# Recurrence gates as products of 64 rows in both halves of the rows, and the heads' sums of squares by high and low part

## The reference

```python
xb = uc.reshape(B, T, 16, 64)                      # 16 blocks of 64 channels
r_gate = sigmoid(einsum('btnc,ncd->btnd', xb, w_r) + b_r)
i_gate = sigmoid(einsum('btnc,ncd->btnd', xb, w_i) + b_i)
log_a = -8.0 * r_gate * softplus(-lru_lambda); a = exp(log_a)
u = sqrt(-expm1(2 * log_a)) * (i_gate * uc)        # then h_t = a_t h_{t-1} + u_t
...
o = attention(q1, q2, k1, k2, v)                   # 8 heads of 128 values
o = o * rsqrt(mean(o * o, axis=-1) + EPS) * g_sub  # per head: the sum of squares
```

## Time and profile before

| | us |
|---|---|
| median of 3 runs | 1968.31 |
| lowest and highest run | 1966.69, 1970.43 |
| the profiled execution | 1966.05 |
| its span from first to last instruction | 1963.2 |
| mean granted TensorE clock in it | 0.996 of full speed |
| PE busy | 1920.9 (98%) |
| DVE busy | 1277.0 (65%) |
| ACT busy | 1061.2 (54%) |
| POOL busy | 191.1 (10%) |

### The profile page before, as it was taken

How to read it: one execution, slowest core, us unless ns; L and a number is a source line. 1 busy time by engine, 2 the same in 40 slices (tenths; PEclk the granted TensorE clock), 3 DMA queues, 4 the chain that set the end, 5 groups by cost and what they waited for, 6 DMA issues and landing times.

```text
span 1963.2 us, 37319 instructions
## 1 busy us (share of the span) xinstructions
PE 1920.9 (98%) x15214; PEld 1880.6 (96%) x15214; DVE 1277.0 (65%) x2334; ACT 1061.2 (54%) x1715; POOL 191.1 (10%) x242
## 2 busy tenths in 40 slices
PE   7999999999999999999999999999999999999997
PEld 7999999999998999999989999999999999999997
DVE  6667676765437766666667676767644388666666
ACT  6466666665236644444565757575732475444445
POOL 4312121100110000000041212120001000000000
PEclk9999999999999999999999999999999999999998
DMA  5323232222332332333313232322232323332221
GB/s 140 105 66 108 71 96 71 85 76 75 93 101 65 99 95 87 86 97 96 98 55 101 66 105 70 103 81 75 76 86 86 97 71 92 92 112 88 87 90 65
DMA packets 275709, 172.32 MB, mean 88 GB/s; under 512 B 7592, under 2 KB 271104, under 8 KB 275552
## 3 DMA queue, kind: packets, MB, share of 16 engines
q1 hardware_dynamic: 268000, 155.47, 27.0%
q0 software_dynamic: 7520, 14.59, 2.4%
q10 hardware_dynamic: 32, 0.04, 0.0%
HBM read 158.86 MB, written 11.21 MB: 87 GB/s over the span
## 4 chain that ended last, share of the span: by engine, by line
PE 87%; ACT 6%; DVE 4%; issue 2%; DMA 0%; SPq 0%; ACTq 0%; DVEq 0%
PE PJ L778 37%; PE PJ L1054 19%; PE PX L1115 13%; PE PJ L960 5%; PE PJ L790 3%; PE PX L989 2%; PE PX L1007 1%; PE PX L902 1%; PE PX L1027 1%; ACT w_hi L1286 1%; PE PX L790 1%; DVE T L1951 1%; PE PX L892 1%; DVE Y L1873 1%; DVE X L1876 1%
## 5 line engine op out<-in xcount | busy, mean ns | idle before, releaser
L1841 DVE TENSOR_TENSOR w_lo<-w_raw,w_hi 128x1024 fp32r<-128x1024 f32 x236 | 299.1, 1269 | 187.7 <-ACT w_hi L1286 186.6
L1286 ACT ACTIVATE w_hi<-w_raw 128x1024 fp32r<-128x1024 f32 x236 | 247.4, 1052 | 204.4 <-DMA w_raw<-in_w_down 120.3
L778 PE MATMUL PJ<-h_hi,w_hi 128*128 128x272 f32 x1536 | 328.4, 295 | 2.6 <-DVE T L1951 1.9
L778 PE MATMUL PJ<-h_hi,w_lo 128*128 128x272 f32 x1536 | 316.6, 288 | 0.0
L778 PE MATMUL PJ<-h_lo,w_hi 128*128 128x272 f32 x1536 | 315.9, 287 | 0.0
L778 PEld LDWEIGHTS PJ<-h_hi,w_hi 128*128 128x128 f32 x1536 | 239.5, 189 | 10.8 <-issue 8.8
L778 PEld LDWEIGHTS PJ<-h_lo,w_hi 128*128 128x128 f32 x1536 | 240.4, 188 | 0.0
L778 PEld LDWEIGHTS PJ<-h_hi,w_lo 128*128 128x128 f32 x1536 | 240.0, 189 | 0.0
L1054 PE MATMUL PJ<-u_hi,w_hi 128*128 128x272 f32 (+2 forms) x1016 | 215.8, 288 | 0.0
L1054 PE MATMUL PJ<-u_hi,w_lo 128*128 128x272 f32 (+2 forms) x1016 | 214.3, 288 | 0.0
L1054 PE MATMUL PJ<-u_lo,w_hi 128*128 128x272 f32 (+2 forms) x1016 | 213.9, 287 | 0.0
(11 more groups left out here) (409 smaller groups left out, 4760.9 us busy)
## 6 DMA issues: line engine op xcount, KB each, us to landing
w_raw<-in_w_in SPq DMA_DIRECT2D x110, 512.0 KB, 3.7
w_raw<-in_w_down SPq DMA_DIRECT2D x64, 512.0 KB, 3.6
w_raw<-in_w_up SPq DMA_DIRECT2D x62, 512.0 KB, 5.2
w_raw<-in_w_branch_attn SPq DMA_DIRECT2D x16, 512.0 KB, 3.6
w_raw<-in_w_branch_lru SPq DMA_DIRECT2D x16, 512.0 KB, 3.6
w_raw<-in_w_out SPq DMA_DIRECT2D x16, 512.0 KB, 3.6
out_prompt_k<-stage POOLq DMA_DIRECT2D x16, 256.0 KB, 2.8
out_prompt_v<-GA POOLq DMA_DIRECT2D x8, 512.0 KB, 5.6
```

What stands on the lines that cost most here:

```text
L778: mm = pe.matmul(PJ[:, buf, half, 0:HT], w[a], src[b][:, k0 + k, HT * half:HT * half + HT], start=first and k == 0 and a + b == 0, stop=en ...
L1286: act.activation(w_hi[:, n.hi, :, :], raw(n), ACT.Copy).then_inc(w_hi_ready, 1)
L1841: dve.tensor_tensor(low(n)[:], raw(n), w_hi[:, n.hi, :, :].bitcast(F32), ALU.subtract).then_inc(w_lo_ready, 1)
```

## The change

- `w_gate` becomes [128, u, 128]: in the rows of block b (64 b on) lie its two weight matrices side by side, r in columns 0 to 63 and i in 64 to 127 for b = 0, the other way round for b = 1. `gates` makes a product of 64 rows for each b and half, into bank 2b + half. So r stands in one half of the partitions for b = 0 and in the other for b = 1, and `gate_acts` has two activations of 64 partitions for each of tr and ti. Both of them read all four banks, so `turn_k` waits for one more step of ACT.
- The bias of i is needed on the other half of the partitions: `bi_cross`, made once on DVE in `first_bias`. The zeros of `w_gate` and their memset on POOL go.
- `sub_square` squares twice, to `sq_hi` (F32R) and `sq_o`; `square_rest` on DVE makes `sq_lo` in the place of `sq_o`, ahead of each `lru_a`; `sub_ssq` makes two products for each half with `ones_r` and waits for `square_rest`. `pv_hi` and `pv_lo` lie elsewhere, to make room.

```diff
@@ -152,7 +152,8 @@
         rs = sb("rs", [P, NT])
         last = sb("last", [P, 2, 8, KT])
-        w_gate = sb("w_gate", [P, 2, 2, P])
+        w_gate = sb("w_gate", [P, 2, P])
+        bi_cross = sb("bi_cross", [P, 2, KT])
         T = sb("T", [P, 2, NT])
@@ -197,6 +199,8 @@
         stage = at("stage", [P, 2, 5, P], F32, S_AT + 4096)
         sq_o = at("sq_o", [P, NT], F32, S_AT + 9216)
+        sq_lo = at("sq_lo", [P, NT], F32R, S_AT + 9216)
+        sq_hi = [at("sq_hi0", [P, NT], F32R, S_AT + 9216 + TILE), at("sq_hi1", [P, NT], F32R, BIG + (4 * KT - 1) * TILE)]
         rr_end = at("rr_end", [P, NT], F32, S_AT + 9216 + TILE)
@@ -625,7 +630,6 @@
                 pool.dma_start(rows[16 * l + R_CW:16 * l + R_CW + 4, :], A["conv_w"][l]).then_inc(small_landed, 16)
                 pool.dma_start(rows[16 * l + R_SC:16 * l + R_SC + 3, :], A["state_conv"][l, 0]).then_inc(small_landed, 16)
-            pool.memset(w_gate[:], 0.0).then_inc(wg_zero, 1)
 
@@ -636,13 +640,13 @@
 
                 g = 4 * l + p
-                need(pool, wg_zero, 1)
                 need(pool, gates_done, 2 * g, first=p == 0)
...
                     for j, name in enumerate(("w_rg", "w_ig")):
                         for b in range(2):
-                            pool.dma_start(w_gate[64 * b:64 * b + 64, u, j, 64 * b:64 * b + 64],
+                            at_ = 64 * ((j + b) % 2)
+                            pool.dma_start(w_gate[64 * b:64 * b + 64, u, at_:at_ + 64],
                                            A[name][l, 4 * p + 2 * u + b]).then_inc(wg_landed, 16)
@@ -897,16 +901,21 @@
                 pe.wait_ge(conv_step, 3 * g2 + 3)
                 need(pe, lru_act, 5 * g2, first=p + u == 0)
-                for j in range(2):
-                    for half in range(2):
-                        mm = pe.matmul(PX[:, 2 * j + half, 0:LH], w_gate[:, u, j, :], uc[:, LH * half:LH * half + LH], start=True, stop=True)
+                for half in range(2):
+                    for b in range(2):
+                        r = slice(64 * b, 64 * b + 64)
+                        mm = pe.matmul(PX[:, 2 * b + half, 0:LH], w_gate[r, u, :], uc[r, LH * half:LH * half + LH], start=True, stop=True)
                 mm.then_inc(gates_done, 1)
...
             def sub_ssq(l, p, u):
                 g2 = 2 * (4 * l + p) + u
-                pe.wait_ge(o_squared, g2 + 1)
+                pe.wait_ge(o_sq_split, g2 + 1)
                 pe.wait_ge(lru_act, 5 * g2 + 2)
-                ones_sum(sq_o, 2).then_inc(o_ssq, 1)
+                for half in range(2):
+                    c = slice(HT * half, HT * half + HT)
+                    pe.matmul(PX[:, 2 + half, 0:HT], ones_r[:], sq_hi[p // 3][:, c], start=True, stop=False)
+                    mm = pe.matmul(PX[:, 2 + half, 0:HT], ones_r[:], sq_lo[:, c], start=False, stop=True)
+                mm.then_inc(o_ssq, 1)
 
@@ -915,7 +924,7 @@
                 need(pe, k_staged, 2 * g + m, first=p + m == 0)
                 if p > 0:
-                    pe.wait_ge(lru_act, 10 * g - 9 + 5 * m)
+                    pe.wait_ge(lru_act, 10 * g - 8 + 5 * m)
                 for grp in range(5):
@@ -1497,9 +1506,14 @@
                 need(act, lru_step, 12 * g2, first=p + u == 0)
                 need(act, pv_lo_ready, 4 * l + p + 2 if p < 3 else 0)
+                act.wait_ge(bi_crossed, DEPTH)
                 for j, t in enumerate((tr, ti)):
-                    act.activation(t[:].rearrange("p (a b) -> p a b", a=2), PX[:, 2 * j:2 * j + 2, 0:LH], ACT.Tanh, scale=0.5,
-                                   bias=gain(l, f, R_BR + j)).then_inc(lru_act, 1)
+                    for b in range(2):
+                        to, by = 64 * b, 64 * ((j + b) % 2)
+                        i = act.activation(t[to:to + 64, :].rearrange("p (a b) -> p a b", a=2), PX[by:by + 64, 2 * b:2 * b + 2, 0:LH],
+                                           ACT.Tanh, scale=0.5,
+                                           bias=bi_cross[by:by + 64, l, f:f + 1] if j else gain(l, f, R_BR)[by:by + 64, :])
+                    i.then_inc(lru_act, 1)
 
@@ -1515,6 +1529,7 @@
                 act.wait_ge(o_placed, NW * (4 * l + p + 1))
                 need(act, o_ssq, g2, first=p + u == 0)
+                act.activation(sq_hi[p // 3][:], O[:, 2 * p + u, :], ACT.Square)
                 act.activation(sq_o[:], O[:, 2 * p + u, :], ACT.Square).then_inc(o_squared, 1)
@@ -2017,6 +2032,11 @@
             def first_bias():
 
+                for l in range(DEPTH):
+                    dve.tensor_copy(bi_cross[0:64, l, :], par[64:P, :, 16 * l + R_BI])
+                    dve.tensor_copy(bi_cross[64:P, l, :], par[0:64, :, 16 * l + R_BI]).then_inc(bi_crossed, 1)
+                dve.wait_ge(ident_ready, 1)
+                dve.tensor_scalar(ones_r[:], ident[:], 0.0, 1.0, ALU.mult, ALU.add)
                 dve.tensor_scalar(bias_s[:, 0, :], bias_s[:, 1, :], -0.5 / SCALE, None, ALU.mult)
@@ -2118,6 +2138,10 @@
                 dve.tensor_copy(last[:, l, 6:7, f], tm[:, PR + NP_ - 1:PR + NP_]).then_inc(lru_step, 1)
                 dve.tensor_copy(last[:, l, 7:8, f], tm[:, NS - 1:NS]).then_inc(lru_step, 1)
+
+            def square_rest(l, p, u):
+                dve.wait_ge(o_squared, 2 * (4 * l + p) + u + 1)
+                dve.tensor_tensor(sq_lo[:], sq_o[:], sq_hi[p // 3][:].bitcast(F32), ALU.subtract).then_inc(o_sq_split, 1)
 
@@ -2376,6 +2400,7 @@
                             split_lo(pair_tile(l, p, 5))
                         if i == 2 and p > 0:
+                            square_rest(l, p - 1, 0)
                             lru_a(l, p - 1, 0)
@@ -2400,6 +2425,7 @@
                                 past_lo(l, p)
                             else:
+                                square_rest(l, p - 1, 1)
                                 lru_a(l, p - 1, 1)
@@ -2434,6 +2460,7 @@
                         split_lo(gate_b_tile(l, i + 2) if i < 6 else mixer_tile(l, T_WA, 0, i - 6))
                     if i == 2:
+                        square_rest(l, 3, 0)
                         lru_a(l, 3, 0)
@@ -2447,6 +2474,7 @@
                         sub_norm(l, 3, 0)
                     if i == 5:
+                        square_rest(l, 3, 1)
                         lru_a(l, 3, 1)
```

More of the change, by code:

```diff
@@ L190, in hybrid_encoder @@
         q_lo = at("q_lo", [P, 2, NT], F32R, V_AT + 9216)
-        pv_hi = at("pv_hi", [P, 2, 2 * VD], F32R, V_AT + 14336)
-        pv_lo = at("pv_lo", [P, 2, 2 * VD], F32R, V_AT + 16384)
+        pv_hi = at("pv_hi", [P, 2, 2 * VD], F32R, V_AT + 13568)
+        pv_lo = at("pv_lo", [P, 2, 2 * VD], F32R, V_AT + 15616)
+        ones_r = at("ones_r", [P, P], F32R, V_AT + 17664)
         o_hi = at("o_hi", [P, KT, NT], F32R, V_AT)
@@ L264, in hybrid_encoder @@
             sem, ("p_turned", "pt_hi_ready", "pt_lo_ready", "pv_done", "o_placed"))
+        o_sq_split = sem("o_sq_split")
         o_squared, o_ssq, o_rs, o_normed, o_hi_ready, o_lo_ready = map(
             sem, ("o_squared", "o_ssq", "o_rs", "o_normed", "o_hi_ready", "o_lo_ready"))
-        wg_zero, wg_landed, hist_ready, conv_first, conv_step, gates_done, lru_act, lru_step = map(
-            sem, ("wg_zero", "wg_landed", "hist_ready", "conv_first", "conv_step", "gates_done", "lru_act", "lru_step"))
+        bi_crossed, wg_landed, hist_ready, conv_first, conv_step, gates_done, lru_act, lru_step = map(
+            sem, ("bi_crossed", "wg_landed", "hist_ready", "conv_first", "conv_step", "gates_done", "lru_act", "lru_step"))
         gelu_done, ga_done, gb_done, l_hi_ready, l_lo_ready, b_scaled, m_hi_ready, m_lo_ready = map(
```

## The result

The changed kernel takes 2015.7 us (median of 4 runs, 2012.8 to 2016.8) where the kernel before takes 1967.8 beside it: ratio 1.0244, 95% interval 1.0229 to 1.0258. The profiled execution took 2015.04 us, its span 2013.3. It is slower, as forecast, but by 47.9 us and not by 24.9; the range ended at 2004.

What follows compares the result with a forecast made beforehand. Both stretches were taken as bound by TensorE and by the ScalarE and VectorE chain at once. Pairs +16.4, gate-b +5.9 and clock +2.6 made +24.9 us on 1966.05: 1991, put down as 1992; range 1977 to 2004.

Steps and rivals of the forecast that it cites:

- all four waits: TensorE would wait at `v_groups(1)`, `turn_k(1)` (some 1.4 us), tile 6 (1.9 us) and gate-b's sums of squares (3.7 us).
- the tile 6 chain: Pair stretch: tile 6 waits for the V rows' second bank, behind an unbroken ScalarE and VectorE chain; start +2.74 us.
- The slack: Pair stretch: between VectorE's evacuation of the V rows' second bank and tile 6's start, 0.2 us.
- TensorE's gates: Gate products of each unit: 8 instructions in 5 slots of 0.231 us plus 0.40 for the 64-row form, -0.29 us.
- my lower bound: Gate products of each unit: full overlap, 4 slots, 1.32 us, -0.53 us.
- The Tanh step: `gate_acts` on ScalarE: four Tanh in place of two, two more steps of 0.60 us, +1.20 a unit.
- my bound of +1.4: `gate_acts` on ScalarE: most that the added Tanh cost a unit, full durations of 0.70 us, no overlap.
- the 16.4: Six pair stretches, first half of pairs 1 to 3 in two layers: tile 6 +2.74 us each, +16.4 us in all.
- The clock in the pairs: Rival: clock also falls in the pair stretches, 1.7 to 3.4 us each; six falls give 2002 to 2012; chance 0.10.
- the stretch of 14 us: Earlier trace, cited against the clock falling in the pairs: 4.2 us idle spread over 14.0 did not lower it.
- Gate-b: Two stretches of gate-b products finishing pair 3: +5.9 us from `o_lo` 2.94 later, +2.6 us from the clock.
- the 448.7: Gate-b stretch: time in us near which VectorE ends `square_rest(1)`, TensorE standing 3.7 us for it.

Runs made afterwards that it cites:

- after_hoist2: after_places with ScalarE's and VectorE's queues around the recurrence reordered (second unit's squares and Tanh earlier, `sub_norm` later, last head's split earlier): 1951.62 us, ratio 0.9921.
- tanh_order: Kernel before with each gate Tanh cut into two of 64 partitions, both gates' first halves ahead of both second halves: 1994.24 us, ratio 1.0132.
- after_order: after_places with a unit's four Tanh ordered as written half 0 of tr and ti, then written half 1 of both: 2005.40 us, ratio 1.0188.
- after_fill: after_places with twelve unused 272-column products into a free bank ahead of tile 6 in pairs 1 to 3: 1999.61 us, ratio 1.0161.
- after_places: Changed kernel with 960 bytes left free, so that `T` and all tiles behind it lie at the addresses of the kernel before: 2005.48 us, ratio 1.0198.
- before_shift: Kernel before with `par` moved to the end, so that `T` and what follows lie 992 bytes lower, no instruction changed: 1974.61 us, ratio 1.0032.
- gates_diag: Kernel before with each unit's four gate products cut into eight of 64 rows and 64 columns, both Tanh whole: 1973.38 us, ratio 1.0030.

## Why the prediction fell short

- **The places** were right: all four waits, and the tile 6 chain with next to no slack. after_hoist2 shows it from the other side. The slack itself was 0.1 us and not 0.2: where TensorE waits in the changed kernel, tile 6 starts 0.15 us after the end of `GA`, in the kernel before 0.23 to 0.27.
- **TensorE's gates**, the slot count. Four slots and not five: the instructions start in pairs 5 to 7 ns apart in 14 of the 16 units (36 in the other two), so -0.52 a unit, my lower bound. It gave no time, because TensorE waits behind it.
- **The Tanh step, the failed term of the sum.** I took 0.60 from the earlier trace rows, where neighbours cover the same 128 partitions; it is 0.71 to 0.74 where they change the half (tanh_order, after_order). +1.72 a unit instead of +1.20, which was even above my bound of +1.4: the bound gave only the two added steps their full 0.70, but the steps from tr to ti and from ti to the Exp, which were there before, lose their overlap too, so that four steps of 0.73 stand in place of two of 0.60. Twice 0.5 in six pairs is 6.1 of the 7.1 us that the pairs lost beyond the 16.4; the slack makes 0.6 more. The Trainium skill (ScalarE: Activation LUTs, What ACT_TABLE_LOAD costs) says that back-to-back activations overlap by some 93 ns; the traces here agree where the first partition stays (0.60 against 0.70) and not where it changes (0.71 to 0.74).
- **The clock in the pairs** was a rival at 0.10, dismissed with the stretch of 14 us in the earlier trace rows, whose idle time lay in small pieces. Here 2.0 us stood in one piece. The four falls cost 1.6 us each, 6.4 us in this trace, and after_fill shows that they go with that standing.
- **The drift, missed altogether.** No line of the prediction asked what a smaller `w_gate` does to the addresses behind it. It was a term put at nothing without a reason: 10.2 us, the largest single part of the error, shown by after_places and before_shift.
- **Gate-b**: +5.9 and +2.6 forecast, 9.0 measured. The sum is near by luck: with the measured Tanh step the first term would be 2.0 larger, 7.9, which leaves, as an estimate, 1.1 for the clock and not 2.6. And TensorE stood 4.2 us for ti, not 3.7 for `sq_lo`; the 448.7 that the forecast takes for the end of `square_rest` stands in no row.
- The terms that were off, 7.1 + 6.4 + 10.2 + 0.5, make 24.2 us. The measured time lies 23.7 above the forecast.

## What to carry to other kernels

Where an engine is 98% busy and two others feed it with 0.1 us of slack, as here, work taken off the first and put on the others is a loss until the fed work is issued earlier; look for the feeder's idle stretch just ahead of the chain (here 3.38 us) and move the work there in the same change. When a tile's size changes, keep the addresses of what lies behind it, or measure the shift alone, before judging the rest. Price a ScalarE instruction cut in two by partitions at its full duration each time, and take the overlap off its neighbour behind it as well.

## What the runs showed of the hardware that I had not expected

- A shift of the data tiles by 960 or 992 bytes, with the weights where they were, moved the step of 272-column products from 124.54 to 125.70 or 125.30 ns: 10.2 and 6.9 us in this kernel.
- ScalarE's overlap of neighbours (0.70 long, 0.60 apart) goes when either the partitions read or those written change half (0.71 to 0.74 apart); from all 128 to the first 64 it stays (a `w_hi` 1.05 long, the Tanh 0.94 behind its start).
- Float32 products of 64 rows from different halves run fully beside each other, 7 ns apart, also into different partition halves of the same bank (gates_diag), 0.23 us for two instructions of 274 columns. That the two of a pair are of different halves is inferred: the trace gives the shape of each and not its rows.
- TensorE standing still for 2.0 us in one piece, 6 us after another 1.8, took the clock to 0.50 for 3.4 us in three or four of six cases; 0.6 us in its place in none. 2.1 to 2.2 us without the earlier piece did it in one and two of six.
